# A two-block transformer on one core: constants in one load, picks one tile sooner, gate rows broadcast through memory

## The reference

```
mod = silu(c) @ ada_w + ada_b             # 2048 x 12288: shift, scale, gate, twice
h = rms_norm(x) * (1 + sc1) + sh1
y = hybrid_mixer(h)                       # q, k, v, a, g = h @ w_in; attention, conv; @ w_out
x = x + g1 * rms_norm(y)
h = rms_norm(x) * (1 + sc2) + sh2
x = x + g2 * rms_norm(swiglu_ffn(h))
# second block: the same frame, with 16-head neighbourhood attention that also
# looks at 256 context tokens, and a gated FFN with a 3-tap convolution
```

## Time and profile before

| | |
|---|---|
| median of 3 runs | 2589.51 us (2588.34 to 2589.73) |
| the profiled execution, its time / its span | 2587.09 us / 2585.4 us |
| mean granted TensorE clock | 0.996 of 2.4 GHz |
| moved by DMA | 619.58 MB, 240 GB/s over the span |
| gate broadcasts start at (us) | 269.5, 716.7, 1245.9, 2099.3 |
| first read by DVE after them (L1775) | 441.0, 1116.7, 1816.9, 2477.8 |

### The profile page before, as it was taken

How to read it: one execution, slowest core, us unless ns; L and a number is a source line. 1 busy time by engine, 2 the same in 40 slices (tenths; PEclk the granted TensorE clock), 3 DMA queues, 4 the chain that set the end, 5 groups by cost and what they waited for, 6 DMA issues and landing times.

```text
span 2585.4 us, 37987 instructions
## 1 busy us (share of the span) xinstructions
PE 2515.3 (97%) x13318; PEld 2085.2 (81%) x13318; DVE 1825.3 (71%) x2258; ACT 1292.6 (50%) x1852; POOL 170.8 (7%) x287
## 2 busy tenths in 40 slices
PE   6999989899999999999999999999999999999999
PEld 5777877787888888887788888887888888888887
DVE  3349888777998888988755565555688866667565
ACT  2349755634444444465534242425566555655454
POOL 0012100231210000000101010100000000000000
PEclk9999999999999999999999999999999999999999
DMA  8989578699987888797454545454478865656554
GB/s 350 388 330 372 197 273 298 195 327 337 306 295 248 284 264 286 271 315 277 152 190 155 187 155 187 155 187 139 155 269 289 269 188 185 186 168 206 195 193 165
DMA packets 219536, 619.58 MB, mean 240 GB/s; under 512 B 20740, under 2 KB 26020, under 8 KB 208672
## 3 DMA queue, kind: packets, MB, share of 16 engines
q1 hardware_dynamic: 205648, 554.76, 62.8%
q0 software_dynamic: 12816, 60.64, 6.6%
q10 hardware_dynamic: 960, 2.70, 0.3%
HBM read 612.25 MB, written 5.77 MB: 239 GB/s over the span
## 4 chain that ended last, share of the span: by engine, by line
PE 78%; DVE 8%; DMA 7%; issue 3%; ACT 3%; SPq 0%; DVEq 0%; ACTq 0%; POOL 0%; POOLq 0%
PE ps L2369 12%; PE ps L2309 11%; PE ps L2311 11%; PE ps L2310 11%; PE ps L2371 6%; PE ps L2742 5%; PE ps L2743 5%; PE ps L2744 5%; DVE w_lo L1434 2%; DMA raw<-in_w_down 2%; PE ps L2344 2%; PE ps L2346 2%; PE ps L2348 2%; DMA ada<-in_ada_w 2%; ACT w_hi L794 1%
## 5 line engine op out<-in xcount | busy, mean ns | idle before, releaser
L1434 DVE TENSOR_TENSOR w_lo<-raw,w_hi 128x1024 fp32r<-128x1024 f32 x762 | 928.4, 1226 | 497.8 <-ACT w_hi L794 496.3
L794 ACT ACTIVATE w_hi<-raw 128x1024 fp32r<-128x1024 f32 x762 | 803.5, 1058 | 896.4 <-PE ps L2311 375.5
L2369 PE MATMUL ps<-h_both,w_hi 128*128 128x512 f32 (+1 forms) x1392 | 485.3, 394 | 1.8 <-DVE h_both L1519 0.8
L2309 PE MATMUL ps<-w_hi,h_both 128*128 128x512 f32 x1152 | 461.7, 401 | 7.5 <-DVE h_both L1519 5.5
L2311 PE MATMUL ps<-w_hi,h_both 128*128 128x512 f32 x1152 | 449.6, 390 | 0.0
L2310 PE MATMUL ps<-w_lo,h_both 128*128 128x512 f32 x1152 | 449.1, 390 | 0.0
L2371 PE MATMUL ps<-h_both,w_lo 128*128 128x256 f32 (+1 forms) x1392 | 388.5, 279 | 0.0
L2369 PEld LDWEIGHTS ps<-h_both,w_hi 128*128 128x128 f32 x1392 | 261.0, 188 | 63.2 <-DVE h_both L1519 1.4
L1446 DVE SCALAR_TENSOR_TENSOR acc<-ada,cact,acc 128x1024 f32<-128x1024 f32 x224 | 290.4, 1296 | 4.6 <-DMA acc<-in_b_ada 1.9
L2742 PE MATMUL ps<-w_hi,f_hi 128*128 128x512 f32 x680 | 265.1, 390 | 1.2 <-DVE z_up L2185 0.8
L2309 PEld LDWEIGHTS ps<-w_hi,h_both 128*128 128x128 f32 x1152 | 216.5, 188 | 61.0 <-issue 7.4
(11 more groups left out here) (282 smaller groups left out, 3055.9 us busy)
## 6 DMA issues: line engine op xcount, KB each, us to landing
ada<-in_w_ada SPq DMA_DIRECT2D x192, 512.0 KB, 4.3
raw<-in_ffn_w_up SPq DMA_DIRECT2D x160, 512.0 KB, 4.4
raw<-in_na_w_qkv SPq DMA_DIRECT2D x96, 512.0 KB, 4.8
raw<-in_w_gate SPq DMA_DIRECT2D x88, 512.0 KB, 5.0
raw<-in_w_up SPq DMA_DIRECT2D x88, 512.0 KB, 4.9
raw<-in_w_down SPq DMA_DIRECT2D x88, 512.0 KB, 5.6
raw<-in_ffn_w_down SPq DMA_DIRECT2D x86, 512.0 KB, 4.5
raw<-in_w_in_tiles SPq DMA_DIRECT2D x80, 512.0 KB, 6.8
```

The costliest lines, as they stand in the source:

```text
L794: act.activation(w_hi[:, s, :], raw[:, s, :], ACT.Copy).then_inc(hi_ready, 1)
L1434: dve.tensor_tensor(w_lo[:, s, :], raw[:, s, :], w_hi[:, s, :].bitcast(F32), ALU.subtract).then_inc(lo_ready, 1)
L2309: pe.matmul(o, hi_[:, k, a], wh, start=(k == 0), stop=False)
L2369: pe.matmul(ps[:, 4 * part + g, :].rearrange("p (a n) -> p a n", a=2)[:, :, n], w_hi[:, s, a], h_both[:, :, k, n], start=(k == 0 and ts[-1 ...
```

## The change

Six edits, all but the last in the first 150 us:

1. `ident`, `ones`, `vecs`, `bias_c` and a new column `pick_1` (1 on partitions 0, 32, 64, 96) are one input of 128 x 401 values, loaded by one transfer on ACT's queue. POOL's steps that built them are gone.
2. x comes as two transfers, token half 1 first, with a semaphore each.
3. The first two eighths no longer begin with a product of `ident` and `ada_rows`, which wrote all rows of the bank; DVE clears banks 6 and 7 instead, and PE waits for `ada_rows` (bias rows of later sums) only after the rounds.
4. PE's rounds: groups first, then tile 3e - 3, groups, tile 3e - 2 with the picks, tile 3e - 1. The first two eighths have an order of their own. SP, ACT and DVE follow.
5. POOL no longer waits for the eighth `h_lo` before `cvec`, `fcw` and the slots of groups 32 and 33; these wait for groups 28 and 29.
6. `broadcast_gate` stores the four pieces to memory by four transfers, waits for them, and loads the row back for all 128 partitions by one transfer of 1 MB.

```diff
-            sp.dma_start(x[:, :, :], ins["x"][0].rearrange("(t p) d -> p t d", p=P)).then_inc(x_landed, 16)
+            for t in (1, 0):
+                sp.dma_start(x[:, t, :], ins["x"][0, t * P:(t + 1) * P, :]).then_inc(x_landed[t], 16)
...
             for n in range(3):
                 mixer_tile(n)
-            for e in range(1, EIGHTHS):
+                if n < 2:
+                    first_group(4 + n)
+            first_group(6)
+            first_group(7)
+            for n in range(3, 6):
+                mixer_tile(n)
+            for e in range(2, EIGHTHS):
                 first_group(4 * e)
                 first_group(4 * e + 1)
                 mixer_tile(3 * e)
...
+                n = gates[0]
+                gates[0] += 1
                 for c in range(4):
-                    gates[0] += 1
-                    pool.partition_broadcast(acc0[:, c * C:(c + 1) * C], row[32 * c:32 * c + 1, :]).then_inc(gate_ready, 1)
-                    pool.wait_ge(gate_ready, gates[0])
-
-            pool.wait_ge(hlo_ready, EIGHTHS)
-            pool.dma_start(cvec[:, :], ins["conv_columns"]).then_inc(small_landed, 16)
-            pool.dma_start(fcw[:, :, :], ins["ffn_conv_columns"]).then_inc(small_landed, 16)
+                    pool.dma_start(gate_d[n, c:c + 1, :], row[32 * c:32 * c + 1, :]).then_inc(gate_stored, 16)
+                pool.wait_ge(gate_stored, 64 * gates[0])
+                pool.dma_start(acc0[:, :], gate_d[n:n + 1].rearrange("o c n -> o (c n)").to_broadcast([P, D])).then_inc(gate_ready, 16)
+
             for g in range(START_GROUPS, GROUPS):
                 group(g)
+                if g == START_GROUPS + 1:
+                    pool.dma_start(cvec[:, :], ins["conv_columns"]).then_inc(small_landed, 16)
+                    pool.dma_start(fcw[:, :, :], ins["ffn_conv_columns"]).then_inc(small_landed, 16)
...
-            act.dma_start(vecs[:, :], ins["vector_columns"]).then_inc(vec_landed, 16)
-            act.dma_start(bias_c[:, :, :], ins["first_bias_columns"]).then_inc(vec_landed, 16)
+            act.dma_start(consts[:, :], ins["constants"]).then_inc(consts_landed, 16)
...
-            act.wait_ge(xt_used, 8)
             for e in range(EIGHTHS):
-                if e:
+                if e >= 2:
                     hi(T_AG, 3 * e)
                 evacuate_sums(e)
+                if e == 0:
+                    act.wait_ge(xt_used, 2)
+                elif e % 2 == 0:
+                    act.wait_ge(xt_used, e + 2)
                 start_hi(e)
...
             all_of(pick_columns(0))
             pe.wait_ge(rstd_read, 1)
-            for e in range(1, EIGHTHS):
+            start_tile(0)
+            group(4)
+            group(5)
+            start_tile(1)
+            group(6)
+            group(7)
+            start_tile(2, pick_columns(1, 10))
+            for e in range(2, EIGHTHS):
                 n, g = 3 * e - 3, 4 * e
-                start_tile(n)
                 group(g)
                 group(g + 1)
-                start_tile(n + 1)
+                start_tile(n)
                 group(g + 2)
                 group(g + 3)
-                start_tile(n + 2, pick_columns(e, 10))
+                start_tile(n + 1, pick_columns(e, 10))
+                start_tile(n + 2)
+
+            pe.wait_ge(sel_ready, 1)
+            pe.wait_ge(const_ready, 3)
+            pe.wait_ge(rows_landed, 16)
```

More of the change, by code:

```diff
@@ L163, in program @@
         S0 = 202 * KB
[L164 to L175, removed]
+        consts = at("consts", [P, 401], S0)
+        ident, ones, vecs = consts[:, 0:128], consts[:, 128:256], consts[:, 256:368]
+        bias_c, pick_1 = consts[:, 368:400].rearrange("p (a k) -> p a k", a=2), consts[:, 400:401]
+        cact = at("cact", [P, 48], S0 + 1632)
+        fcw = at("fcw", [P, 4, 86], S0 + 1824)
+        qg = at("qg", [P, HD], S0 + 3200)
+        kg = at("kg", [P, HD], S0 + 3712)
+        cols = at("cols", [P, 10, KD], S0 + 4224)
+        stat = at("stat", [P, 64], S0 + 4864)
+        eps_rms = at("eps_rms", [P, 1], S0 + 5120)
+        eps_ln = at("eps_ln", [P, 1], S0 + 5152)
         tab = at("tab", [DR * H2, LANES], S0 + 5184)
@@ L221, in program @@
         acc_bias = [sem(f"acc_bias{i}") for i in range(3)]
-        vec_landed = sem("vec_landed")
+        consts_landed = sem("consts_landed")
+        banks_clear = sem("banks_clear")
         small_landed = sem("small_landed")
-        x_landed = sem("x_landed")
+        x_landed = [sem(f"x_landed{t}") for t in range(NT)]
         ctx_landed = sem("ctx_landed")
@@ L619, in link @@
                 pool.wait_ge(pool_step, steps[0])
-            link(pool.memset(ident[:, :], 0.0))
             pool.memset(eps_rms[:, :], RMS_EPS)
             pool.memset(eps_ln[:, :], LN_EPS)
[L624 to L627, removed]
+            pool.memset(zero[:, :], 0.0).then_inc(const_ready, 1)
             pool.memset(mean1[:, :], 1.0 / (H1 * HD)).then_inc(const_ready, 1)
@@ L2527, in group @@
                     pe.wait_ge(tr_free[b], m_)
-                if g % 4 == 0 and e < 2:
-                    pe.matmul(ps[:, 6 + b, :], ident[:, :], ada_rows[:, :], start=True, stop=False)
                 pe.wait_ge(first_landed[slot], 16 * slot_uses(g))
@@ L2535, in group @@
                                    slots[slot][:, r // 2, r % 2 * EC:(r % 2 + 1) * EC],
-                                   start=(e >= 2 and g % 4 == 0 and r < 4), stop=(sec == 1 and half == 1 and r >= 4))
+                                   start=(g % 4 == 0 and r < 4), stop=(sec == 1 and half == 1 and r >= 4))
                 mm.then_inc(group_done, 1)
@@ L2545, in pick_columns @@
                 for o in range(4):
-                    mm = pe.matmul(ps[:, 6 + b, o:o + 1], sums[:, o * P:(o + 1) * P], pick[:, 28:29], start=True, stop=True)
+                    mm = pe.matmul(ps[:, 6 + b, o:o + 1], sums[:, o * P:(o + 1) * P], pick_1[:, :], start=True, stop=True)
                     if o == 3:
@@ L2615, in _ @@
             group(1)
+            group(2)
             x_columns(6, 8)
-            group(2)
             group(3)
```

61 lines of the change are left out of this document (29 added, 32 removed).

## The result

The changed kernel takes 2571.02 us (median of four runs, 2568.32 to 2572.53) against 2589.25 of the kernel before: ratio 0.9929, 95% interval 0.9912 to 0.9946. That is 18.2 us, where the sum came to 11.6. In two further series on other occasions the change was worth 15.7 and 18.8 us. The direction was forecast, and so was what the head and the rounds win; the time lies at the lower edge of the range because the term for POOL's queue failed, and because the clock and the part behind 150 us gave more than was summed.

What follows compares the result with a forecast made beforehand. PE, busy 97% of the span, was taken as the bound, so only its idle time could be won. 6.5 + 1.0 + 9.0 - 0.3 - 1.4 - 4.5 + 1.0 + 0.3 = 11.6 us gave 2577.9, range 2571 to 2583.

Steps and rivals of the forecast that it cites:

- Head, 6.5 us: Program start: constants by DMA and x in halves let tile 0 start at 26.4 in place of 32.92, gaining 6.5 us.
- Rounds, 9.0 - 0.3: Seven rounds: picks in the second tile remove waits of 1.29 us, gaining 9.0, less 0.3 once at tile 3.
- 1.0 for the preload: Opening: two PSUM preloads go, the second of which stood between tiles; gain 1.0 us.
- 1.4 for DMA: Rounds: at 412 GB/s the last slot, group 31, lands later than PE wants it; loss 1.4 us.
- POOL's queue, 4.5 us: Near 113 us: POOL's early 2.4 MB hold up SP's last slots, for which PE waits; loss 4.5, bounds 0 and 5.8.
- After the opening, 1.0 us: Group 35's wait of 1.19 us at 164.66 shrinks; gain 1.0 us, bounds 0 and 1.2.
- the gates, 0.3 us: Gate broadcasts by store and load in place of POOL: gain 0.3 us, between +1.3 and -1.2.
- the good bound: Best case at the gates, a gain of 1.3 us, where PE had waited 1.20 us for DVE.
- The rule on loads from HBM: Skill's limit of about 358 GB/s per core: a round would take 16.1 us, so rounds could not get shorter.
- rival D: Nothing seen: waits move from `h_lo` to slots and the earlier head is eaten; 2587.5 us, chance 0.07.
- rival B: PE sets the pace: DMA gives 420 GB/s or more, or SP's slots are not held up; near 2572, chance 0.27.

Runs made afterwards that it cites:

- r_before: The kernel before, run again unaltered against itself: gain -1.2 us, ratio 0.9998.
- e11: The kernel before with the first three gate rows stored and loaded back, only the last broadcast by POOL: gain 2.1 us, ratio 0.9988 against the kernel before.
- e4: The changed kernel with the gate rows broadcast by POOL again: gain 16.6 us, ratio 0.9938 against the kernel before.
- e12: The kernel before with the new head alone (constants by DMA, halves of x, no PSUM preload): gain 8.1 us, ratio 0.9959 against the kernel before.
- r2_after: The changed kernel run again unaltered in a later series: gain 18.8 us, ratio 0.9931 against the kernel before.
- e10: The changed kernel with the two small constants early and POOL's slots late: gain 17.4 us, ratio 0.9933 against the kernel before.
- e9: The changed kernel with slots of groups 32 and 33 early, small constants behind group 34's slot: gain 19.4 us, ratio 0.9923 against the kernel before.
- r_after: The changed kernel run again unaltered: gain 15.7 us, ratio 0.9936 against the kernel before.

## Why the prediction was off

By its own steps:

- **Head, 6.5 us.** Right on the profile it was made from: 32.92 to 26.50. The constants landed at 7.00 and not at 9.4, and as said that added nothing. Not foreseen is the clock: in two of the three profiles where POOL's stall stands ahead of the old head (r_before, e11), a low clock costs 1.6 to 2 us more at tile 0 and 2.2 at the end of the rounds; the new head has no wait for `ada_rows`, and none of its profiles has that loss. Over the two profiles of before that is 1.1 us on the mean. The reason given was incomplete: I read the 10.54 us on POOL as the cost of building `ident` there, where it is the cost of a broadcast elsewhere in the program.
- **Rounds, 9.0 - 0.3 + 1.0 for the preload, less 1.4 for DMA.** With the head that is 14.8 us at the end of the rounds; the version without POOL's early requests is at 147.79 - 133.18 = 14.6. DMA gave 416 GB/s for the 412 assumed; the remainder went into small waits for slots near 44 and 50 and into tile 3.
- **POOL's queue, 4.5 us.** This step failed. It let POOL's 2.4 MB share DMA with SP's last slots from 113 on, and had PE wait 3 to 6 us for group 30 or 31. PE waited at most 0.3 us there, in three profiles. POOL issued at 114.43, and its first bytes moved at 118; till then SP's queue had 97 to 100% of the DMA time, and by 118 its last slots were in. What was held up were the tiles behind them: 2.3 us at the end of the rounds, of which 0.2 are left at 260 when the clock stays up. I had costed the transfer against the wrong victim.
- **After the opening, 1.0 us, and the gates, 0.3 us.** These were mis-sized together. Between the end of the rounds and the table load of the next phase (274.78 and 276.78 before; 258.15, 260.88 and 258.30 after) the means give another 16.7 - 13.5 = 3.2 us, 1.9 more than the 1.3 summed. Slot waits went from 3.0 us to 1.1 on the mean, all over this stretch and not at group 35 alone; the other 1.3 us were not traced. At the gate PE's wait of 1.20 us is gone with no tile delayed, as the good bound had it, but it lies behind this landmark, and the spans differ by only 0.5 us more (17.2 against 16.7). The split of 1.69 us beside the broadcast is in no other profile with a broadcast there (1.21 in r_before, e4 and e12); the products of 128x256 beside it take 0.88 us in place of 0.48 in all four. (The third and fourth gate are first read at 1815.8 and 2472.4; the table of before gives the last reads. Nothing changes by it.)
- **The rule on loads from HBM** named in the prediction, and with it rival D, is out for this kernel on its one core: the windows above have 416 to 421 GB/s.
- **The range.** Its upper end was added up wrong: 11.6 less 2.1 (403 GB/s), 2 (clock) and 1.5 (gate) is a gain of 6.0 us, not 6.7.

2.2 for POOL's queue, 1.1 for the clock, 1.9 behind 150 us: 11.6 + 5.2 = 16.8, against 17.2 between the means of two spans before (2585.4, 2589.4) and three after (2570.6, 2572.2, 2567.8). In its time the outcome is rival B, but that is partly luck. B had DMA at 420 or more or SP's slots not held up. The slots were not, but DMA's loss of 1.4 was there as forecast and the tiles cost 2.3; the clock (1.1) and the stretch behind 150 (1.9) made up for most of it: 17.5 - 1.4 - 2.3 + 1.1 + 1.9 = 16.8. Of the late scatter of some 3 us, 1.7 is the clock behind the wait at tile 24; which transfer makes the slot waits is open.

## What to carry to other kernels

Read an idle time whose end is "issue" as a cost of its own, and ask what else in the program could bring it, before you put it down to the instruction behind it. Where two edits of a change remove the same stall, undo each alone and do each alone: undone alone the gates cost about 1 us, done alone they won 8.6. And when a transfer is sent earlier beside others, count what is still outstanding by the time its bytes move, not when it is issued; then look for the loss at the next transfers in line. Take a second profile of either kernel before you explain 2 us: here the clock behind one wait moved them.

## What was new about the hardware

- One gate's four calls of `partition_broadcast` anywhere in the program make POOL stand still for 10.3 to 14.1 us ahead of its first instruction beyond memsets and DMA issues, in all five profiles of a program with such calls (before twice, e4, e11, e12). In the twelve profiles without them the gap is 0.24 us or less. Ahead of the first gate's calls there is one more, of 8.9 to 12.3 us (before twice, e4, e12), and behind them one of 6.8 to 8.1; in e11, where POOL had waited for 213 us, the call began 0.15 us after its data. The Trainium skill, GPSIMD Engine Reference, "2.1 Instruction dispatch", has about 6 us for code loaded at a first call; all gaps at the start and ahead of the first gate's calls are longer than that. What POOL does in them no trace shows.
- DMA moved 417 GB/s over the 110 us from 10 to 120, in each of the three profiles of the changed kernel.
- Where both queues had work, POOL's moved 67 packets with 0.55 MB and SP's 81 with 0.29 MB in the same 2 us (118 to 120): nearly equal in packets, unequal in bytes. The queue with the longer lines gets the larger part. The Trainium skill, DMA: Bandwidth & Descriptors, "Queues, rings and completion order", has each engine take the queues in turn packet by packet, and the nearly equal counts agree with it.
- A request of POOL's moved its first bytes some 1.3 us after its issue where DMA was idle (before, issued at 141.16), and 3.7 us after where SP's queue filled it.
- A wait of 1.43 us on PE left the clock at full speed, one of 2.0 us at the same place was followed by some 3 us near 1.2 GHz, in each of the two profiles that have it. But the length of the wait does not decide it: at tile 24, waits of 2.72 us (first profile of the changed kernel), 2.91 (r2_after), 2.83 (e10) and 3.20 (e4) left the clock at full speed, and waits of 2.49 (e9) and 3.22 us (r_after) were followed by some 3 us near 1.2 GHz, which cost 1.7 us.
